# Marks of scores unlike the threshold, made by GpSimd in two passes ahead of use instead of by VectorE in one

## The chip, the core and the metric

The kernel runs on one core of a Trainium2 chip. The metric is the device time of one execution in microseconds (us), the median over runs. In the profile PE is TensorE's matmul, PEld its weight load, DVE is VectorE, ACT is ScalarE and POOL is GpSimd; a name such as L1752 is a line of the kernel.

## The reference, cut to what matters

Two transformer-like blocks follow one another on one sequence of 1024 tokens, width 1024, in float32. The change lies in the first, in its sparse attention. An indexer gives each pair of query and key a score; each query keeps the 256 keys of highest score among those not after it (`lax.top_k`, which takes the earlier key where scores are equal), and softmax attention of 8 heads runs over those keys alone:

```python
score = jnp.where(causal[None], score, -jnp.inf)
_, idx = lax.top_k(score, topk)                  # topk = 256
sel_ok = idx <= t_pos[None, :, None]
kg = jax.vmap(lambda kb, ib: kb[ib])(k, idx)     # the kept keys, vg likewise
logits = jnp.einsum('btkgd,btjkd->btkgj', qg, kg) * (HEAD_DIM ** -0.5)
p = jax.nn.softmax(jnp.where(sel_ok[...], logits, -jnp.inf), axis=-1)
o = jnp.einsum('btkgj,btjkd->btkgd', p, vg)
```

A second branch, the gated one, gives the other half of the features; both halves are normalised, joined and go through the output projection and a feed-forward network of width 4096.

## The kernel before

`select_and_gate` finds the threshold of every query by a search over its bits and leaves it in `found`, one column for each of the six query blocks in `SCORED = [7, 6, 5, 4, 3, 2]`. A query block is 128 queries; block b sees (b + 1) * 128 keys, so the six have 1024, 896, 768, 640, 512 and 384 keys. Blocks 1 and 0 need no selection.

`attend` then does the attention. It works through `order = [1] + SCORED + [0]`, eight blocks of eight heads, as 64 steps (block, head), two steps at a time. Each engine has its own program of these steps, and semaphores join them:

- TensorE, for the pair p: the `logits` of both heads into PSUM (two steps share four banks, so those of steps i wait for the masking of steps i - 2), `turn` (transposes of the probabilities of pair p - 1, which reuse a PSUM bank that VectorE or ScalarE must have copied out), a quarter of the `values` product of the block before, and at set pairs the transposes `by_token` and `turn_y` of a finished block. In the first four pairs it also sums the squares of the gated branch (`sum_gated`, L1651).
- VectorE, in `mask(i)` (L1771), adds the block's row of `never` to the logits, scales, and takes the row's extreme; it copies the transposed probabilities of odd steps out of PSUM (L1814), and it does the selection, `select(j, part)`, one part a step during block j of the order, one block before the block's own masks: part 0 counts scores above the threshold (L1746), part 1 makes in `equal` a mark for each score unlike the threshold (L1749), part 2 runs a scan over these marks that ranks the ties (L1752), parts 3 and 4 (L1754, L1757) turn rank and score into the block's row of `never`. Its other work on a block that is through: `divide`, `mean`, `scale` (L1796), `store`. All of it stands in one queue.
- ScalarE takes the exponentials (L1692) and copies the even steps' transposed probabilities.
- GpSimd multiplies the gated branch by its gain (four instructions, L1572) and by its inverse root (four, L1578), and raises each block's mean square to the power -0.5 (L1584). VectorE's `scale(a)` waits for that power. `mean(a)` comes right behind `select(a + 2, 4)` in VectorE's queue, `scale(a)` one step later, behind one copy of probabilities.

`equal` is one buffer for all six blocks. `wait_ties(eng, a)` waits until part 4 of the selection `a` has run. A barrier stands between attention and the next stage (at 470 us).

Of the kernel before, what the change touches and what calls it, by code (L numbers as in the profile page):

```python
# [15 lines left out]
P = 128  # L16
# [25 lines left out]
AWAY = -2.0 ** 100  # L42

F32 = mybir.dt.float32
# [1414 lines left out]
def attend(nc, K, rot, val, never, found, out, gated):  # L1459
# [29 lines left out]
    with ExitStack() as ctx:  # L1489
# [11 lines left out]
        power = K.sbuf(ctx, "power", [P, 1])  # L1501
        away = K.sbuf(ctx, "away", [P, 1])
        (logits_ready, logits_masked, exp_done, p_turned, copied_by_act, copied_by_dve, pv_ready, y_evicted, y_by_token,
         sum_inverted, y_made, y_squared, mean_made, inverted, y_scaled, y_turned, y_stored, power_set, gain_taken) = (K.flag(n).sem for n in (
             "logits_ready", "logits_masked", "exp_done", "p_turned", "p_copied_by_act", "p_copied_by_dve", "pv_ready",
             "y_evicted", "y_by_token", "sum_inverted", "y_made", "y_squared", "y_mean_made", "y_inverted", "y_scaled",
             "y_turned", "y_stored", "power_set", "gated_gain_taken"))
        psum = K.psum
        p_copied = (copied_by_act, copied_by_dve)
        gated_squares = turned[:, 1].rearrange("p k g j t -> p (k g j t)")[:, 0:4 * S].rearrange("p (t s) -> p t s", t=4)  # L1510
# [22 lines left out]
                return []  # L1533
            return [n for n in range(bank_of[(i, 0)], last_bank[i] + 1) if copier(n) == who]

        tie_steps, before_ties = 6, K.dve_done.n + 1

        def wait_ties(eng, a):

# [21 lines left out]
        with nc.Block(no_gpsimd_drain=True) as block:  # L1561
            @block.gpsimd
            def _(pool):
                for h in range(2):
                    half = gated[:, 3, h * HALF:(h + 1) * HALF]
                    pool.tensor_tensor(out=half, in0=out[:, 0, h * HALF:(h + 1) * HALF], in1=half, op=ALU.mult) \
                        .then_inc(K.pool_done.sem, 1)
                pool.memset(power[:], -0.5).then_inc(power_set, 1)
                wait_ties(pool, 0)
                for t in range(4):  # L1570
                    pool.wait_ge(gated_squared.sem, gated_squared.n + t + 1)
                    pool.tensor_scalar(gated[:, t, :], gated[:, t, :], K.col("g_out_sgu", t), None, op0=ALU.mult) \  # L1572
                        .then_inc(gain_taken, 1)
                pool.wait_ge(gated_rooted.sem, gated_rooted.n + 2)
                wait_ties(pool, 1)
                for t in range(4):
                    pool.wait_ge(gain_taken, t + 1)
                    pool.tensor_tensor(out=gated[:, t, :], in0=gated[:, t, :], in1=gated_root, op=ALU.mult) \  # L1578
                        .then_inc(gated_normed.sem, 1)
                pool.wait_ge(power_set, 1)  # L1580
                for a in range(NT):
                    m = ms[:, a % 2:a % 2 + 1]
                    pool.wait_ge(mean_made, a + 1)
                    pool.tensor_tensor(out=m, in0=m, in1=power[:], op=ALU.pow).then_inc(inverted, 1)  # L1584

# [149 lines left out]
            @block.vector  # L1735
            def _(dve):
                c = Chain(dve, K.dve_done)
                selected = []
                c(dve.memset(away[:], AWAY))

                def select(j, part):

                    s, n = never[:, score_at(SCORED[j]):score_at(SCORED[j] + 1)], (SCORED[j] + 1) * P
                    found_j, same, at = found[:, j:j + 1].bitcast(F32), equal[:, 0:n], rank[:, 0:n]
                    if part == 0:
                        c(dve.tensor_scalar(above[:, 0:n], s, found_j, None, op0=ALU.is_gt, op1=ALU.add,  # L1746
                                            accum_out=count[:]))
                    if part == 1:
                        c(dve.tensor_scalar(same, s, found_j, AWAY, op0=ALU.not_equal, op1=ALU.mult))  # L1749
                    if part == 2:  # L1750
                        c(dve.tensor_scalar(need[:], count[:], -AWAY, AWAY * TOPK, op0=ALU.mult, op1=ALU.add))
                        c(dve.tensor_tensor_scan(at, away[:].broadcast_to([P, n]), same, 0.0, ALU.add, ALU.subtract))  # L1752
                    if part == 3:
                        c(dve.scalar_tensor_tensor(out=same, in0=at, scalar=need[:], in1=same, op0=ALU.subtract,  # L1754
                                                   op1=ALU.min))
                    if part == 4:
                        c(dve.scalar_tensor_tensor(out=s, in0=s, scalar=found_j, in1=same, op0=ALU.is_le, op1=ALU.mult))  # L1757
                        selected.append(c.n)
                        assert c.n == before_ties + tie_steps * (j + 1)

                def mask(i):
                    b, u = steps[i]
                    a, n = i // HEADS, (b + 1) * P
                    if u == 0 and b in SCORED:
                        c.wait(selected[a - 1])
                    dve.wait_ge(logits_ready, i + 1)
                    if i == 2:
                        dve.wait_ge(K.pool_done.sem, K.pool_done.n)
                    if i >= COPIES:
                        dve.wait_ge(p_turned, last_bank[i - COPIES] + 1)  # L1770
                    dve.tensor_tensor_reduce(out=logit[:, i % COPIES, 0:n], in0=keys(logit_banks(i)[0], n),  # L1771
                                             in1=never[:, score_at(b):score_at(b + 1)], scale=-HD ** -0.5,
                                             scalar=3.0e38, op0=ALU.add, op1=ALU.min,
                                             accum_out=low[:, a % 2, u:u + 1]).then_inc(logits_masked, 1)

                def divide(a):
                    dve.wait_ge(exp_done, HEADS * (a + 1))
                    dve.reciprocal(total[:, a % SUMS, :], total[:, a % SUMS, :]).then_inc(sum_inverted, 1)
                    dve.wait_ge(y_by_token, a + 1)
                    dve.wait_ge(sum_inverted, a + 1)  # L1780
                    if a >= 2:
                        dve.wait_ge(y_turned, a - 1)
                    dve.tensor_tensor(out=y[:, a % 2], in0=psum[:, VALUES + a % 2, :].rearrange("p (h d) -> p h d", d=HD),
                                      in1=total[:, a % SUMS, :].unsqueeze(2).broadcast_to([P, HEADS, HD]), op=ALU.mult) \
                        .then_inc(y_made, 1)

                def mean(a):
                    m = ms[:, a % 2:a % 2 + 1]
                    dve.wait_ge(y_squared, a + 1)
                    dve.tensor_scalar(m, m, 1.0 / (HEADS * HD), EPS, op0=ALU.mult, op1=ALU.add).then_inc(mean_made, 1)  # L1790

                def scale(a):
                    m = ms[:, a % 2:a % 2 + 1]
                    dve.wait_ge(inverted, a + 1)
                    flat = y[:, a % 2].rearrange("p h d -> p (h d)")
                    dve.tensor_scalar(flat, flat, m, None, op0=ALU.mult).then_inc(y_scaled, 1)  # L1796

                def store(a):
                    b = order[a]
                    dve.wait_ge(y_turned, a + 1)  # L1800
                    dve.tensor_tensor(out=out[:, :, b * P:(b + 1) * P],
                                      in0=psum[:, VALUES + a % 2, :].rearrange("p (j t) -> p j t", t=P),
                                      in1=K.col("g_out_attn", 0, 4).unsqueeze(2).broadcast_to([P, 4, P]),
                                      op=ALU.mult).then_inc(y_stored, 1)

                for i in range(len(steps) + 10):
                    if i < len(steps) and i % 2 == 0:
                        mask(i)
                        mask(i + 1)
                    if i % 2:  # L1810
                        for n in copies_of(i - 2, 1):
                            to, of = turned_bank(n)
                            wait_turned(dve, n)
                            dve.tensor_copy(to, of).then_inc(copied_by_dve, 1)  # L1814
                    if i // HEADS < len(SCORED):
                        select(i // HEADS, i % HEADS)
                    for a in due(i, DIVIDE, HEADS):
                        divide(a)
                    for a in due(i, MEAN, HEADS):
                        mean(a)  # L1820
                    for a in due(i, SCALE, HEADS):
                        scale(a)
                    for a in due(i, STORE, HEADS):
                        store(a)
                K.dve_done.n = c.n
# [4023 lines left out]
```

## Time and profile before

| | |
|---|---|
| median of 3 runs | 2730.77 us (2730.49 to 2733.97) |
| the profiled execution, its own time | 2734.42 us |
| its span | 2732.7 us |
| mean granted TensorE clock | 0.996 |
| busy: PE, PEld, DVE, ACT, POOL | 2653.1, 2098.8, 1877.9, 1336.1, 264.2 us |
| attention (`attend`) | 323 to 470 us of the span |
| busy there: PE, DVE, ACT, POOL | 137.23, 115.86, 89.53, 27.82 us of 147 |

The time of an execution is the span and 1.7 us around it. Busy shares are averages over stages with different limits; what a change in attention is worth is read from attention's own stretch. Ends of matmuls are modelled, so a busy PE is not PE at its peak. In a row of the timeline the bracket gives the idle time just before, and who ended it.

### The profile page before, as it was taken

The numbers are of one execution on the slowest core, as the hardware profiler recorded it, in microseconds if no ns is written. First come the engines' busy times: TensorE is split into PE (matmuls) and PEld (weight loads), VectorE is DVE, ScalarE is ACT, GpSimd is POOL, SyncE is SP. The second block draws the span as 40 slices with busy tenths as digits, with TensorE's granted clock in tenths as the row PEclk, the third lists the DMA queues.
The fourth block names the chain that finished last, engine by engine and source line by source line (L and its number), as shares of the span: only waits on it lengthen the run. The fifth ranks groups of instructions, "written<-read, shape, count | busy, mean of one in ns | idle before, by whom it ended". The sixth has DMA issues, their size and how long they took to land.

```text
span 2732.7 us, 41783 instructions
## 1 busy us (share of the span) xinstructions
PE 2653.1 (97%) x16684; PEld 2098.8 (77%) x16684; DVE 1877.9 (69%) x2861; ACT 1336.1 (49%) x1979; POOL 264.2 (10%) x390
## 2 busy tenths in 40 slices
PE   7999999999999999999999999989999999999998
PEld 4758755877888888867778898768788878888886
DVE  7889887568665476784987616767565666646676
ACT  4359665587555434464441115453334655543444
POOL 0126520011000000000000002110000100000000
PEclk9999999999999999999999999999999999999999
DMA  7621101365666888722464332216344656687874
GB/s 292 223 89 35 41 1 38 133 213 191 229 231 225 304 284 293 257 110 66 132 163 134 139 131 87 80 45 199 105 149 159 219 201 231 227 303 257 298 279 153
DMA packets 211121, 474.39 MB, mean 174 GB/s; under 512 B 49712, under 2 KB 70832, under 8 KB 205648
## 3 DMA queue, kind: packets, MB, share of 16 engines
q1 hardware_dynamic: 193392, 394.91, 43.7%
q0 software_dynamic: 17536, 76.82, 7.1%
q8 instruction: 132, 2.16, 0.3%
q14 instruction: 61, 0.50, 0.1%
HBM read 344.09 MB, written 124.29 MB: 171 GB/s over the span
## 4 chain that ended last, share of the span: by engine, by line
PE 73%; DVE 5%; ACT 2%; issue 2%; SPq 1%; DMA 1%; ACTq 0%; DVEq 0%
PE psum L2335 44%; PE psum L3890 11%; PE psum L2273 4%; PE psum L5470 3%; PE psum L4301 3%; PE psum L4961 2%; PE psum L4370 1%; PE psum L2281 1%; PE psum L3898 1%; SPq L5169 1%; DMA g_a<-ssm_gate_dram 1%; DVE merged L2887 0%; DVE x L2891 0%; PE psum L2260 0%; PE psum L4435 0%
## 5 line engine op out<-in xcount | busy, mean ns | idle before, releaser
L2335 PE MATMUL psum<-merged_operand 128*128 128x512 f32 x1536 | 360.8, 390 | 0.0
L2335 PEld LDWEIGHTS psum<-merged_operand 128*128 128x128 f32 x1536 | 288.5, 188 | 60.5
L2335 PE MATMUL psum<-h_half_operand 128*128 128x512 f32 x1344 | 316.8, 391 | 0.0
L2335 PEld LDWEIGHTS psum<-h_half_operand 128*128 128x128 f32 x1344 | 252.4, 188 | 55.3 <-issue 1.0
L2335 PE MATMUL psum<-h_half_operand,weight_parts_operand 128*128 128x512 f32 x768 | 177.8, 392 | 0.9 <-DVE weight_parts_operand L2859 0.6
L2335 PEld LDWEIGHTS psum<-h_half_operand,weight_parts_operand 128*128 128x128 f32 x768 | 143.5, 188 | 34.5 <-DVE weight_parts_operand L2859 3.3
L3890 PE MATMUL psum<-x_operand,weight_high 128*128 128x512 f32 x432 | 135.6, 395 | 0.0
L2859 DVE TENSOR_TENSOR weight_parts_operand<-weight_ring,weight_parts_operand 128x1024 fp32r<-128x1024 f32 x65 | 79.5, 1222 | 80.7 <-ACT weight_parts_operand L2501 80.5
L3890 PE MATMUL psum<-o_operand,weight_high 128*128 128x512 f32 x432 | 133.5, 390 | 0.0
L3890 PE MATMUL psum<-x_operand,weight_low 128*128 128x512 f32 x432 | 133.1, 389 | 0.0
L2859 DVE TENSOR_TENSOR h_half_operand<-hidden_upper,h_half_operand 128x1024 fp32r<-128x1024 f32 (+1 forms) x58 | 74.1, 1297 | 72.7 <-ACT h_half_operand L2636 51.9
L2859 DVE TENSOR_TENSOR h_half_operand<-o,h_half_operand 128x1024 fp32r<-128x1024 f32 (+1 forms) x58 | 74.1, 1297 | 71.8 <-ACT h_half_operand L2636 51.0
L2859 DVE TENSOR_TENSOR merged_operand<-o,merged_operand 128x1024 fp32r<-128x1024 f32 (+1 forms) x50 | 64.3, 1309 | 59.9 <-ACT merged_operand L2636 53.2
L2501 ACT ACTIVATE weight_parts_operand<-weight_ring 128x1024 fp32r<-128x1024 f32 x61 | 64.4, 1056 | 81.0 <-PE psum L2273 41.2
L2859 DVE TENSOR_TENSOR merged_operand<-hidden_upper,merged_operand 128x1024 fp32r<-128x1024 f32 (+1 forms) x50 | 64.3, 1308 | 57.4 <-ACT merged_operand L2636 51.0
L3890 PEld LDWEIGHTS psum<-x_operand,weight_high 128*128 128x128 f32 x432 | 79.7, 188 | 28.6 <-issue 13.2
L2335 PE MATMUL psum<-x_operand,merged_operand 128*128 128x512 f32 x384 | 93.4, 392 | 1.4 <-issue 1.4
L3890 PEld LDWEIGHTS psum<-x_operand,weight_low 128*128 128x128 f32 x432 | 81.1, 188 | 17.3
L3890 PEld LDWEIGHTS psum<-o_operand,weight_high 128*128 128x128 f32 x432 | 81.1, 188 | 17.0
L1351 DVE TENSOR_SCALAR_CACHE_REDUCE above<-score,test_bits 128x768 uint8<-128x768 f32 (+3 forms) x114 | 88.1, 826 | 7.3 <-DVE test_bits L1377 7.3
L2335 PE MATMUL psum<-x_operand,h_half_operand 128*128 128x512 f32 x384 | 92.4, 390 | 0.0
L215 DVE CAST weight_high<-weight_ring 128x1024 fp32r<-128x1024 f32 (+1 forms) x43 | 25.5, 594 | 95.0 <-PE psum L3890 58.9
(689 smaller groups left out, 5935.4 us busy)
## 6 DMA issues: line engine op xcount, KB each, us to landing
o<-in_w_ff SPq DMA_DIRECT2D x80, 512.0 KB, 4.5
merged<-hidden_terms SPq DMA_DIRECT2D x56, 512.0 KB, 6.0
hidden_upper<-in_w_ff_down SPq DMA_DIRECT2D x48, 512.0 KB, 4.7
weight_ring<-in_w_out SPq DMA_DIRECT2D x32, 512.0 KB, 3.4
hidden_terms<-weight_parts POOLq DMA_DIRECT2D x16, 1024.0 KB, 8.0
hidden_terms<-weight_ring POOLq DMA_DIRECT2D x16, 1024.0 KB, 7.6
hidden_upper<-in_w_ff_up SPq DMA_DIRECT2D x32, 512.0 KB, 4.6
o<-hidden_terms SPq DMA_DIRECT2D x28, 512.0 KB, 5.9
```

The source lines that it names most:

```text
L1351: counted[j % 2] = c.step(dve.tensor_scalar(above[:, j % 2, 0:(SCORED[j] + 1) * P], keys(j), limit, None, op0=op, op1=ALU.add, accum_out=c ...
L2273: mm = pe.matmul(mix_bank(i), w[:, at], h, start=(k == 0 and m == 0), stop=(k == KT - 1 and m == 2))
L2281: return pe.matmul(mix_bank(i), w[:, k * P:(k + 1) * P], h, start=start, stop=stop)
L2335: mm = pe.matmul(bank, w[:, at:at + P], tiles(r, i), start=opens and m == 0, stop=closes and m == 2, skip_group_check=resumed)
L2501: act.activation(w_high(n), K.ring[:, n % RING, :], ACT.Copy).then_inc(w_rounded.sem, 1)
L2859: return dve.tensor_tensor(out=low, in0=of, in1=plain(high), op=ALU.subtract)
L3890: mm = pe.matmul(banks(n)[:, g, :], w[:, cols], x[:, k, at(g)], start=(k == 0 and m == 0), stop=(k == KT - 1 and m == 2))
L3898: mm = pe.matmul(banks(n)[:, g, :], w[:, cols], x[:, k, at(g)], start=(k == 0 and m == 0), stop=(k == KT - 1 and m == 2))
L4301: mm = pe.matmul(out(k, odd, j), left(k, odd, j), moving(k, odd, j), start=True, stop=True)
L4370: mm = pe.transpose(psum[:, 2, j * P:(j + 1) * P], flat(T[:, n % 2, 2 * j:2 * j + 2, :]), K.const("ident"))
L4961: mm = pe.matmul(K.psum[:, m, :], x[:, k, j:S:BLOCK], w[:, :, at], start=(i == 0 and part == 0), stop=(i == KT - 1 and part == 2))
L5470: return pe.matmul(acc(n)[:, h, :], left[:, n % 2, k * P:(k + 1) * P], x[:, k, h * HALF:(h + 1) * HALF], start=first, stop=last)
```

## The change

VectorE's part 1 (L1749) goes. GpSimd gets a function `mark_unlike(j)` of two dependent passes over the block's scores: the first writes 0 where the score is the threshold and -1 elsewhere, the second multiplies by `-AWAY`, which gives the same marks. It waits for the selection j - 1 to have ended, since `equal` is one buffer, and VectorE's part 2 waits for the second pass. In GpSimd's queue the calls for j = 0 and 1 stand ahead of the gain's multiplications, j = 2 ahead of the root's, and j = 3, 4, 5 each ahead of the power for a = 0, 1, 2. VectorE's selection now counts five instructions instead of six.

```diff
-        tie_steps, before_ties = 6, K.dve_done.n + 1
+        tie_steps, before_ties = 5, K.dve_done.n + 1
...
             @block.gpsimd
             def _(pool):
+                def mark_unlike(j):
+                    if j:
+                        wait_ties(pool, j - 1)
+                    s, n = never[:, score_at(SCORED[j]):score_at(SCORED[j] + 1)], (SCORED[j] + 1) * P
+                    pool.tensor_scalar(equal[:, 0:n], s, found[:, j:j + 1].bitcast(F32), 1.0, op0=ALU.is_equal,
+                                       op1=ALU.subtract).then_inc(unlike_marked, 1)
+                    pool.wait_ge(unlike_marked, 2 * j + 1)
+                    pool.tensor_scalar(equal[:, 0:n], equal[:, 0:n], -AWAY, None, op0=ALU.mult).then_inc(unlike_marked, 1)
+
...
                 pool.memset(power[:], -0.5).then_inc(power_set, 1)
-                wait_ties(pool, 0)
+                mark_unlike(0)
+                mark_unlike(1)
                 for t in range(4):
                     pool.wait_ge(gated_squared.sem, gated_squared.n + t + 1)
                     pool.tensor_scalar(gated[:, t, :], gated[:, t, :], K.col("g_out_sgu", t), None, op0=ALU.mult) \
                         .then_inc(gain_taken, 1)
                 pool.wait_ge(gated_rooted.sem, gated_rooted.n + 2)
-                wait_ties(pool, 1)
+                mark_unlike(2)
...
                 for a in range(NT):
                     m = ms[:, a % 2:a % 2 + 1]
+                    if a + 3 < len(SCORED):
+                        mark_unlike(a + 3)
                     pool.wait_ge(mean_made, a + 1)
                     pool.tensor_tensor(out=m, in0=m, in1=power[:], op=ALU.pow).then_inc(inverted, 1)
...
-                    if part == 1:
-                        c(dve.tensor_scalar(same, s, found_j, AWAY, op0=ALU.not_equal, op1=ALU.mult))
                     if part == 2:
+                        dve.wait_ge(unlike_marked, 2 * j + 2)
                         c(dve.tensor_scalar(need[:], count[:], -AWAY, AWAY * TOPK, op0=ALU.mult, op1=ALU.add))
                         c(dve.tensor_tensor_scan(at, away[:].broadcast_to([P, n]), same, 0.0, ALU.add, ALU.subtract))
```

## Rows read from the trace of the kernel before

**Rows 1.** Windows of attention: us, busy time and instructions of each engine, granted clock, DMA.
```profile
360.00:376.00 16.00, 16.00 (x95) 8.48 (x94) 15.07 (x26) 10.86 (x22) 5.04 (x3) 1.00 0.00 1
```

**Rows 2.** Waits in attention: who waited for whom, us, times, longest.
```profile
DVE p_turned_sbuf L1814 <- PE psum L1613: 9.7, 12, 1.9
...
PE psum L1613 <- DVE p_turned_sbuf L1814: 1.4, 2, 0.8
```

**Rows 3.** GpSimd's groups by shape: count, busy us, mean ns, idle before.
```profile
L1249 POOL TENSOR_SCALAR marks<-score,test_bits 128x384 f32<-128x384 f32 x10 | 12.5, 1249 | 12.4 <-DVEq L1434 12.4
L1572 POOL TENSOR_SCALAR merged<-merged,cols 128x1024 f32<-128x1024 f32 x4 | 11.3, 2839 | 8.2 <-DVE score L1757 8.2
...
L4850 POOL COPY t<-eye 128x512 f32<-128x512 f32 x8 | 5.3, 668 | 3.7 <-PE psum L4301 3.7
```

**Rows 4.** Line 1749 on VectorE: count, shortest/median/longest ns, first and last start.
```profile
L1749 DVE TENSOR_SCALAR equal<-score,found_bits x6: 408/578/1558, 326.1 to 425.2; 128x1024 f32<-128x1024 f32 x1, 128x896 f32<-128x896 f32 x1, 128x768 f32<-128x768 f32 x1, 128x640 f32<-128x640 f32 x1
```

**Rows 5.** GpSimd's timeline early in attention: start, us, operation, idle before.
```profile
325.52 0.10 POOL L1568 MEMSET power<- 128x1 f32 x1
333.81 11.31 POOL L1572 TENSOR_SCALAR merged<-merged,cols 128x1024 f32<-128x1024 f32 x4 [8.19 <-DVE score L1757]
355.68 9.37 POOL L1578 TENSOR_TENSOR merged<-merged,q_k_qi_ki 128x1024 f32<-128x1024 f32 x4 [10.56 <-issue]
376.51 0.59 POOL L1584 TENSOR_TENSOR mean_square<-mean_square,power 128x1 f32<-128x1 f32 x1 [11.47 <-DVE mean_square L1790]
```

**Rows 6.** VectorE's timeline, first block to be selected.
```profile
327.57 0.15 DVE L1751 TENSOR_SCALAR ties_needed<-count 128x1 f32<-128x1 f32 x1
327.76 2.29 DVE L1752 TENSOR_TENSOR_SCAN rank<-away,equal 128x1024 f32<-128x1024 f32 x1
```

**Rows 7.** TensorE's timeline, 330 us: two transposes of probabilities.
```profile
330.65 0.41 PE L1613 MATMUL psum<-consts,q_k_qi_ki 128*128 128x128 f32 x2 [0.85 <-DVE p_turned_sbuf L1814]
```

**Rows 8.** VectorE's timeline, 375 to 419 us: selection, scaling, last mask, three times.
```profile
375.17 1.01 DVE L1757 SCALAR_TENSOR_TENSOR score<-score,found_bits,equal 128x768 f32<-128x768 f32 x1
...
377.37 0.48 DVE L1796 TENSOR_SCALAR y_by_token<-y_by_token,mean_square 128x512 f32<-128x512 f32 x1
...
378.77 1.08 DVE L1771 CUSTOM_DVE_ANT_0 q_k_qi_ki<-psum,score 128x896 f32<-128x896 f32 x1
...
396.10 0.88 DVE L1757 SCALAR_TENSOR_TENSOR score<-score,found_bits,equal 128x640 f32<-128x640 f32 x1
...
398.03 0.48 DVE L1796 TENSOR_SCALAR y_by_token<-y_by_token,mean_square 128x512 f32<-128x512 f32 x1
...
399.30 0.95 DVE L1771 CUSTOM_DVE_ANT_0 q_k_qi_ki<-psum,score 128x768 f32<-128x768 f32 x1
...
415.04 0.75 DVE L1757 SCALAR_TENSOR_TENSOR score<-score,found_bits,equal 128x512 f32<-128x512 f32 x1
...
416.71 0.48 DVE L1796 TENSOR_SCALAR y_by_token<-y_by_token,mean_square 128x512 f32<-128x512 f32 x1
...
418.00 0.82 DVE L1771 CUSTOM_DVE_ANT_0 q_k_qi_ki<-psum,score 128x640 f32<-128x640 f32 x1
```

**Rows 9.** TensorE's timeline, the logits after each of those masks.
```profile
381.24 1.56 PE L1599 MATMUL psum<-q_k_qi_ki 64*128 64x512 f32 x8
...
401.90 1.35 PE L1599 MATMUL psum<-q_k_qi_ki 64*128 64x512 f32 x8
...
419.99 1.13 PE L1599 MATMUL psum<-q_k_qi_ki 64*128 64x512 f32 x4
```

**Rows 10.** Timeline at 1619 us: GpSimd, then VectorE with two SBUF inputs.
```profile
1618.66 2.35 POOL L4856 TENSOR_TENSOR a_off_diagonal<-pairs_and_ends,chunk_consts 128x1024 f32<-128x1024 f32 x1 [3.08 <-DVE pairs_and_ends L4684]
...
1619.31 2.28 DVE L4701 COPY_PREDICATED t<-chunk_consts,a_low 128x512 f32<-128x512 uint32 x1
```

**Rows 11.** TensorE, three windows: us, busy (instructions), granted clock, DMA share, GB/s.
```profile
342.00:348.00 6.00, 2.64 (x17) 0.95 0.00 0
...
348.00:351.00 3.00, 3.00 (x12) 0.52 0.03 5
```

More of the change, by code:

```diff
@@ L1503, in attend @@
         (logits_ready, logits_masked, exp_done, p_turned, copied_by_act, copied_by_dve, pv_ready, y_evicted, y_by_token,
-         sum_inverted, y_made, y_squared, mean_made, inverted, y_scaled, y_turned, y_stored, power_set, gain_taken) = (K.flag(n).sem for n in (
+         sum_inverted, y_made, y_squared, mean_made, inverted, y_scaled, y_turned, y_stored, power_set, gain_taken, unlike_marked) = (K.flag(n).sem for n in (
              "logits_ready", "logits_masked", "exp_done", "p_turned", "p_copied_by_act", "p_copied_by_dve", "pv_ready",
              "y_evicted", "y_by_token", "sum_inverted", "y_made", "y_squared", "y_mean_made", "y_inverted", "y_scaled",
-             "y_turned", "y_stored", "power_set", "gated_gain_taken"))
+             "y_turned", "y_stored", "power_set", "gated_gain_taken", "unlike_marked"))
         psum = K.psum
```

## The prediction

> **What bounds the kernel now.** I read the page first, then attention alone, because the change touches nothing outside 323 to 470 us: its windows, its waits, GpSimd's groups by shape, and the timelines of VectorE, TensorE and GpSimd at the places where a wait is added. In the window of a middle block TensorE is busy throughout, 16.00 of 16 us, and VectorE 15.07 [rows 1]. TensorE's matmuls stand there end to end, so it sets the pace and VectorE follows with little to spare. The waits say the same: VectorE's copies wait 9.7 us for TensorE's transposes, and TensorE waits for such a copy twice, 1.4 us in all [rows 2], one of them the 0.85 us at 330.65 [rows 7]. The barrier behind attention lets nothing overlap, so a microsecond that TensorE loses here is lost at the end. What matters is where VectorE becomes late enough for TensorE to feel it.
>
> **What is removed.** Six marks on VectorE, 408 to 1558 ns with a median of 578 [rows 4]; by the six single times 4.35 us together. All but the first lie where TensorE does not wait for VectorE, so I cost them at nothing; their cover is TensorE's own queue. The bound on the other side is 1 us, for a little slack gained.
>
> **What one pass costs on GpSimd.** The trace has no such two-operation pass. The nearest are the comparison with a per-partition operand over 384 elements, 1249 ns, and the multiplication over 1024, 2839 ns [rows 3]. A line through both is 2.48 ns an element and 0.30 us. By it a pass over 1024, 640, 512 and 384 elements takes 2.84, 1.88, 1.57 and 1.25 us, and the two with 0.1 us between them 5.8, 3.9, 3.2 and 2.6 us. From below, the nearest is the copy of 512 elements at 0.668 us [rows 3], some 1.2 ns an element, if an immediate operand made a pass that cheap. From above I allow the first pass, with two operations, half as much again. I take the line, since both its rows are this very kind of instruction.
> The Trainium skill speaks for the low end: "GPSIMD Engine Reference", section 4.1, has GpSimd at about line rate for one-input work. At one element a cycle of its 1.2 GHz that would be an estimated 0.85 us for 1024 elements; both rows of the kind contradict it by a factor near three.
>
> **Term 1, the first block.** GpSimd's queue reaches the marks behind the memset, at 325.6 us [rows 5]. Two passes of 1024 end at 331.4. VectorE's part 2 then needs 0.2 us for its small instruction, and the scan starts at 331.65 instead of 327.76 [rows 6]: 3.9 us later, with the removed mark already counted. "One block ahead" holds from the second block on; the first has no block before it. Queued behind the waiting part are the copy of step 1, parts 3 and 4, and the masks of steps 4 and 5. TensorE's transpose at 330.65 waits for that very copy [rows 7], so it is late by the same amount, and everything behind it on three engines. From 3.9 us the bounds are 0.5 (both passes as the copy) and 5.3.
>
> **Term 2, the power behind the marks.** For a = 0, 1, 2 GpSimd must now do `mark_unlike(a + 3)` before the power, and may start it only when selection a + 2 has ended. VectorE's `scale(a)` waits for the power and comes one step behind that selection. For a = 0 the selection ends at 376.2 and `scale` starts at 377.37 [rows 8]. GpSimd would start at 376.3, mark until 380.15, and give the power (0.59 us before [rows 5]) at 380.8: VectorE stands 3.4 us. For a = 1 the selection ends at 397.0, the power comes at 400.95 and `scale` was due at 398.03: 2.9 us. For a = 2 it is 415.8, 419.1 and 416.71: 2.4 us [rows 8].
> Behind `scale` in VectorE's queue stand the two masks whose banks the next logits need. The second of them ends at 379.86, 400.26 and 418.83 with its readout [rows 8]; TensorE's next logits start at 381.24, 401.90 and 419.99 [rows 9], the ones for the second bank 0.15 us later. The slack is 1.5, 1.8 and 1.3 us, and TensorE loses 1.9, 1.1 and 1.1: 4.1 us. At later transposes and copies VectorE is then late by no more than TensorE is. Bounds: 0 (passes as the copy: the first stall is 1.2 us, under its slack) and 6.5 (the two-operation pass half as long again adds 0.9, 0.8 and 0.6).
> The marks for j = 1 to 5 are themselves ready before their scans: for j = 1 at 343 against a scan near 350, the tightest of them, so that added wait costs nothing there. If it did, it would be the scan's delay one for one.
>
> **Term 3, two engines at one port.** A VectorE instruction with two SBUF inputs at 1619 us started 0.65 us behind one of GpSimd's and ended 0.6 us after it; its 2.28 us for 512 elements [rows 10] are twice what the scan takes for an element [rows 6] and seem to be some 1.7 us of standing until GpSimd was through, and 0.6 of work. Before, the gain's four instructions ran at 333.8 to 345.1 and the root's at 355.7 to 365.05 [rows 5], clear of scans. Now they come behind marks: the gain's at about 343 to 354, the root's at about 365 to 375. All of VectorE's clock is then some 5 us later, so the scans of the second and third block, at 346 and 368 before, fall near 351 and 373.5, inside both. Each can be held 0 to 2.8 us. The second block has an idle microsecond behind it; the third has 0.4 us of slack, read as in term 2. I take 1.0 us, bounds 0 and 3.
> The Trainium skill has this as a rule: "SBUF — State Buffer" calls the shared port pair an exclusive lock, held for the whole instruction, and names two SBUF inputs against a GpSimd instruction that reads. The trace agrees, by those 2.28 us.
>
> **Term 4, TensorE's clock.** From 342 to 348 us TensorE was busy only 2.64 of 6 us, and from 348 to 351 its granted clock was 0.52, so 1.2 GHz for most of 3 us, before it rose again to 2.4 [rows 11]. Term 1 makes a new hole, from about 329.8 to 334.6, busy some 1.2 of 6 us around it. I expect the same fall behind it: 3 us at half rate, 1.5 us lost. Bounds: 0 (no fall) and 3.5 (one more behind a stall of term 2).
>
> **The sum.** 3.9 + 4.1 + 1.0 + 1.5 - 0 = 10.5 us. Against the profiled execution's own 2734.42 us that is 2744.9; that execution is 3.65 us over the median of the runs, 2730.77, and against the median it gives 2741.3 us. The other bounds, not all at once, reach from about +1 to about +17.
>
> **The rivals.** A change under 0.2% (5.5 us) can't be told from none here.
> (a) Main: GpSimd's marks cost about as the line says, and the four waits bite; +6 to +16 us, most likely +10.5, 2741.3 us. Chance 0.72.
> (b) Only the second pass, with an immediate, runs at the copy's rate. Each pair is 0.75 to 1.6 us shorter: term 1 is 2.3, term 2 about 1.4, terms 3 and 4 together 1: +4.7, 2735.5 us. For it: no row shows an immediate pass of this size. Against: a comparison and a multiplication cost much the same an element, 3.3 and 2.8 ns with all overheads [rows 3], so what the pass does seems not to matter. Chance 0.11, half of it within 0.2%.
> (c) Both passes near the copy's rate, 1.2 ns an element. Term 1 is 0.6, term 2 nothing, the rest nothing: 2731.4 us, no change. This is the case on the other side; it decides once a pass of 1024 takes less than about 2 us, where terms 1 and 2 together fall to some 3. By the rule of "GPSIMD Engine Reference" of the Trainium skill, named above, this is the case that comes out. Against it stand both rows of the kind. Chance 0.06. A gain over 0.2% would want more than the 4.35 us removed, so it gets 0.02, for a clock fall at 348 us that the new timing spares as well.
> (d) The two-operation pass costs half as much again, or the clock falls after several stalls, or VectorE is held at the port each time: +16 to +22, say 2750 us. Chance 0.09.
>
> **Range and chances.** From 2735 to 2748.5 us; outside it lie (c), the faster case, most of (d), and a tail of (b). Slower by over 0.2%: (a) nearly whole, (d), half of (b): 0.87. Within: 0.11. Faster: 0.02.
>
> **What would show it.** The waits of the profile after should have VectorE waiting for GpSimd's `equal` once, some 4 us, and for `mean_square` three times, 2.4 to 3.4 us each; the marks' groups on GpSimd give the pass's price at once (2.84 us for 1024). The granted clock should fall near 335 us. The barrier should come some 10 us later, and the stages behind it keep their lengths. I am wrong if a pass of 1024 takes much under 2 us (b, c), or if TensorE's idle time in attention grows by much less than VectorE's stalls, which would mean more slack than I read.

## The result and the profile after

The changed kernel takes 2744.92 us in the median of 6 runs (2742.05 to 2751.25), the one before 2732.05 (2730.49 to 2735.29): ratio 1.0047, 95% interval 1.0035 to 1.0059, so 12.8 us slower (9.6 to 16.1). The prediction said 10.5 us slower, 2741.3 us. Its other figure, 2744.9, was counted from the one profiled execution, and that the median came out at the same number is chance; 1.3 of the 3.6 us between 2741.3 and 2744.92 is that the kernel before came out slower in six runs than in the three it was counted from.

The first two lines of the page after, and its busy line: GpSimd has 28.5 us more to do, VectorE 2.7 us less, TensorE the same work.

```profile
span 2740.3 us, 41788 instructions
...
PE 2654.6 (97%) x16684; PEld 2098.1 (77%) x16684; DVE 1875.2 (68%) x2855; ACT 1335.9 (49%) x1979; POOL 292.7 (11%) x402
```

Those 2740.3 us are the span of the fastest of the six runs. It is not the span that tells what the change did, but attention's own length. TensorE's first and last logits there, before and then after (an extract of each timeline: start, duration, what; the bracket is idle time before):

```profile
323.25 0.70 PE L1599 MATMUL psum<-q_k_qi_ki 64*128 64x256 f32 x4 [1.33 <-PEq L1023]
```

```profile
455.90 0.49 PE L1599 MATMUL psum<-q_k_qi_ki 64*128 64x128 f32 x4
```

```profile
321.11 0.70 PE L1611 MATMUL psum<-q_k_qi_ki 64*128 64x256 f32 x4 [1.33 <-PEq L1023]
```

```profile
465.92 0.49 PE L1611 MATMUL psum<-q_k_qi_ki 64*128 64x128 f32 x4
```

From 132.65 to 144.81 us: 12.16 us longer. Attention began 2.1 us earlier in this trace, and what follows it was 2.4 us shorter. Both lie in code that the change does not touch: the start is taken up below, and what follows differs by 3.3 us between the two traces of the kernel before itself.

The waits in attention, as in [rows 2] (who waited for whom: us, times, longest). Two are new, VectorE for GpSimd's marks (`equal`) and for its power (`mean_square`), and TensorE's wait for VectorE's copies has grown from 1.4 to 6.8 us:

```profile
DVE y_by_token L1807 <- POOL mean_square L1596: 10.4, 5, 3.9
...
PE psum L1625 <- DVE p_turned_sbuf L1825: 6.8, 3, 5.5
...
DVE ties_needed L1762 <- POOL equal L1571: 5.4, 1, 5.4
...
PE psum L1656 <- DVE y_by_token L1807: 1.6, 3, 1.1
```

GpSimd's groups by shape, beside [rows 3] (busy us, mean ns, idle before). L1568 is the first pass, with two operations, L1571 the second, L1582 the gain's multiplication:

```profile
L1582 POOL TENSOR_SCALAR merged<-merged,cols 128x1024 f32<-128x1024 f32 x4 | 12.1, 3042 | 0.1
...
L1568 POOL TENSOR_SCALAR equal<-score,found_bits 128x1024 f32<-128x1024 f32 x1 | 3.7, 3721 | 0.0
...
L1571 POOL TENSOR_SCALAR equal<-equal 128x1024 f32<-128x1024 f32 x1 | 2.8, 2793 | 0.1
...
L1568 POOL TENSOR_SCALAR equal<-score,found_bits 128x640 f32<-128x640 f32 x1 | 2.4, 2431 | 7.9 <-DVE score L1768 7.9
...
L1571 POOL TENSOR_SCALAR equal<-equal 128x640 f32<-128x640 f32 x1 | 1.8, 1816 | 0.1
```

VectorE's timeline where it now waits, beside [rows 6, 8]: the scans of the first three blocks, and the three scalings:

```profile
330.10 0.15 DVE L1762 TENSOR_SCALAR ties_needed<-count 128x1 f32<-128x1 f32 x1 [5.37 <-POOL equal L1571]
330.29 2.29 DVE L1763 TENSOR_TENSOR_SCAN rank<-away,equal 128x1024 f32<-128x1024 f32 x1
...
349.68 2.02 DVE L1763 TENSOR_TENSOR_SCAN rank<-away,equal 128x896 f32<-128x896 f32 x1
...
371.13 3.65 DVE L1763 TENSOR_TENSOR_SCAN rank<-away,equal 128x768 f32<-128x768 f32 x1
...
386.09 0.48 DVE L1807 TENSOR_SCALAR y_by_token<-y_by_token,mean_square 128x512 f32<-128x512 f32 x1 [3.94 <-POOL mean_square L1596]
...
408.67 0.48 DVE L1807 TENSOR_SCALAR y_by_token<-y_by_token,mean_square 128x512 f32<-128x512 f32 x1 [3.26 <-POOL mean_square L1596]
...
428.38 0.49 DVE L1807 TENSOR_SCALAR y_by_token<-y_by_token,mean_square 128x512 f32<-128x512 f32 x1 [2.57 <-POOL mean_square L1596]
```

TensorE behind the first and the second of these waits, beside [rows 7, 9]:

```profile
333.18 0.66 PE L1625 MATMUL psum<-consts,q_k_qi_ki 128*128 128x128 f32 x2 [5.52 <-DVE p_turned_sbuf L1825]
333.64 3.62 PE L1663 MATMUL psum<-p_turned_sbuf,consts 128*128 128x512 f32 x4
...
386.63 0.66 PE L1656 MATMUL psum<-consts,y_by_token 128*128 128x128 f32 x4 [1.06 <-DVE y_by_token L1807]
387.63 2.57 PE L1611 MATMUL psum<-q_k_qi_ki 64*128 64x512 f32 x8 [0.35 <-DVE minus_max L1782]
```

And its windows (us, busy, granted clock, DMA share, GB/s), beside [rows 11]:

```profile
328.00:332.00 4.00, 0.00 (x0) 1.00 0.01 2
333.00:339.00 6.00, 5.82 (x13) 0.50 0.00 0
347.00:353.00 6.00, 2.64 (x21) 1.00 0.00 0
```

Below, a hole is a stretch in which TensorE stands idle, and a fall is one in which its granted clock is 0.50, 1.2 GHz. The reader can follow the loss by the start of each pair's logits, less the first one's, against the same difference before. It is nothing up to the third pair. At the sixth pair it is 6.7 us: the scan came 4.7 us late, TensorE stood 5.52 us at the transpose, and came out of the hole at 1.2 GHz, 0.50 for six microseconds, in which the 512-wide sums at 333.64 took 3.62 us. Then 1.6 us come back: the fall at 348 us before [rows 11] is missing. The third block's scan, 3.65 us where its length is 1.76, adds 1.0 us. The three scalings add 3.5, 1.7 and 1.0. From there on the difference stays 12.15 us to the last logits.

### The profile page after: what moved, and what is told of

Same layout as the page of the kernel before. It is cut to its first block, busy times and chain, and to the rows that moved or that the text cites. A ratio compares the mean times of both kernels' runs of the same rounds, so it can differ in the third digit from the quotient of the medians.

```text
span 2740.3 us, 41788 instructions
## 1 busy us (share of the span) xinstructions
PE 2654.6 (97%) x16684; PEld 2098.1 (77%) x16684; DVE 1875.2 (68%) x2855; ACT 1335.9 (49%) x1979; POOL 292.7 (11%) x402
## 4 chain that ended last, share of the span: by engine, by line
PE 75%; DVE 4%; ACT 2%; issue 1%; ACTq 0%; DVEq 0%
PE psum L2346 44%; PE psum L3901 11%; PE psum L2284 4%; PE psum L5481 3%; PE psum L4312 3%; PE psum L4972 2%; PE psum L5197 1%; PE psum L2292 1%; PE psum L4381 1%; PE psum L3909 1%; DVE merged L2898 0%; DVE x L2902 0%; PE psum L2271 0%; PE psum L4446 0%; PE psum L4436 0%
## 5 line engine op out<-in xcount | busy, mean ns | idle before, releaser
L2346 PEld LDWEIGHTS psum<-h_half_operand,weight_parts_operand 128*128 128x128 f32 x768 | 143.5, 188 | 34.5 <-DVE weight_parts_operand L2870 3.3
```

The source lines that it names most:

```text
L2346: mm = pe.matmul(bank, w[:, at:at + P], tiles(r, i), start=opens and m == 0, stop=closes and m == 2, skip_group_check=resumed)
```

## The experiments

The measure in them is attention's length, from its first logits to its last, by one trace each; the ratio of whole runs stands beside it with its interval. A trace is one execution of several, and need not be a typical one: where the two columns disagree, the text says so.

| kernel | attention, us | against before | ratio of whole runs (95%) |
|---|---|---|---|
| before; again | 132.65; 132.65 | 0 | |
| changed; again; a third time | 144.81; 144.62; 144.65 | +12.16; +11.97; +12.00 | 1.0047 (1.0035 to 1.0059) |
| first block's marks by VectorE; again | 143.46; 138.15 | +10.81; +5.50 | 1.0043 (1.0026 to 1.0060) |
| power ahead of marks | 139.35 | +6.70 | 1.0025 (1.0012 to 1.0037) |
| both | 132.75 | +0.10 | 1.0002 (0.9991 to 1.0012) |
| one pass | 135.87 | +3.22 | 1.0016 (1.0005 to 1.0026) |
| hole filled | 145.43 | +12.78 | 1.0064 (1.0050 to 1.0078) |
| port alone | 136.47 | +3.82 | 1.0020 (1.0010 to 1.0029) |
| before, holes filled | 131.16 | -1.49 | 1.0006 (0.9996 to 1.0017) |
| relief alone | 132.63 | -0.02 | 1.0012 (1.0002 to 1.0021) |

**The first block's marks by VectorE again.**

```diff
-                mark_unlike(0)
...
+                    if part == 1 and j == 0:
+                        c(dve.tensor_scalar(same, s, found_j, AWAY, op0=ALU.not_equal, op1=ALU.mult))
                     if part == 2:
-                        dve.wait_ge(unlike_marked, 2 * j + 2)
+                        if j:
+                            dve.wait_ge(unlike_marked, 2 * j)
```

> The changed kernel, but VectorE makes the marks of the first block itself, as before, so that GpSimd starts with the second. Theory (the waits for GpSimd are the loss, term by term): the stall of 4.7 us at the first scan and the fall of the clock behind it (2.1 us) go, and the fall near 348 us comes back (1.6 us): attention 7.1 us longer than before instead of 12.15. Rival one (the two engines hold each other up at their shared port, wherever GpSimd works beside VectorE): nearly the same GpSimd work is left, so 10 us or more stay.

Up to the sixth pair the starts are those of before: the stall at the scan is gone, as expected. But 10.8 us stayed in this trace, by the clock and not by the port. Its windows show two falls, one 2.5 us ahead of the place of the old one and for 7 us, and one behind the scaling's stall of 3.9 us, which cost 3.2 us more there than the changed kernel lost:

```profile
351.10:355.10 4.00, 3.89 (x14) 0.50 0.02 4
391.10:395.10 4.00, 4.00 (x14) 0.50 0.00 0
```

> Once more the kernel in which VectorE makes the first block's marks. In its first trace attention was 10.8 us longer than before, where 7.1 were expected, with a stretch at 1.2 GHz near 390 us behind the stall of 3.9 us. Theory (that fall wanders): without a fall there, attention is 6 to 8 us longer; with one, 10 to 12. Rival (the stall before the scaling always brings the clock down when nothing fell before it): the same fall at the same place, 10.8 us.

The second trace of the same kernel has no fall in attention at all, and every step but the clock's is the same. It is 5.5 us over before, which had its fall of 1.6 us: 7.1 us where neither falls. That is the 7.1 expected at first; the 6 to 8 us expected of this trace were missed, since they took for granted that the fall near 348 us would be there. Whole runs are on the side of the first trace: the six of this kernel took 2742.2 to 2749.9 us, 1.0043, no better than the changed kernel's 1.0047, and the execution of the second trace, at 2736.25 us, is faster than all of them. So this edit takes away the first stall, and in most executions the clock seems to take the gain back; one trace shows where, and no run shows how often.

```profile
340.00:350.00 10.00, 6.64 (x41) 1.00 0.01 2
380.00:390.00 10.00, 9.53 (x50) 1.00 0.00 0
```

**Each power ahead of the marks.**

```diff
                 for a in range(NT):
                     m = ms[:, a % 2:a % 2 + 1]
-                    if a + 3 < len(SCORED):
-                        mark_unlike(a + 3)
                     pool.wait_ge(mean_made, a + 1)
                     pool.tensor_tensor(out=m, in0=m, in1=power[:], op=ALU.pow).then_inc(inverted, 1)
+                    if a + 3 < len(SCORED):
+                        mark_unlike(a + 3)
```

> The changed kernel, but in GpSimd's last loop each power stands ahead of the marks, not behind them. Theory: the three stalls of 3.9, 3.3 and 2.6 us before the scaling go, with the 6.1 us that TensorE lost by them; the first block's stall and the clock stay: attention 6.1 us longer than before, the scaling never waits for GpSimd over 0.5 us. Rival one (shared port): the marks then run beside VectorE's scaling and copies instead of while it stands still, and 10 us or more stay.

Measured +6.7 us, 5.3 to 5.5 less than the changed kernel's three traces, and whole runs agree (1.0025 is 6.8 us). The waits for the scaling are back at 0.6 us, and the marks are still ready in time:

```profile
DVE ties_needed L1762 <- POOL equal L1571: 5.4, 1, 5.4
...
DVE y_by_token L1807 <- POOL mean_square L1594: 0.6, 2, 0.4
```

It is 0.6 us over the expected 6.1. The starts say why: the third block's scan now costs TensorE 1.75 us (1.0 at once, 0.75 a pair later), where it seemed to cost 1.0 in the changed kernel. The rest had eaten slack that the scaling's stall then missed.

**Both edits.**

> Both edits: VectorE makes the first block's marks, and each power stands ahead of the marks. Theory: what is left is the scan held at the port, 1 us (0 to 3), so within 0.2% of before, and no gain from the 3 us of VectorE's work removed, since TensorE sets the pace. Rival one (shared port): over 5 us slower. Rival two (VectorE's relief is worth something once the stalls are gone): 2 to 3 us faster than before.

+0.10 us, and a ratio of one. In this trace nothing falls near 348 us, so the sum is 1.63 us gained by the clock and 1.75 us lost at the third block's scan. That scan took 3.68 us here and in the kernel above, 1.76 us before; GpSimd's root multiplications (L1587) ran beside it:

```profile
366.18 3.68 DVE L1765 TENSOR_TENSOR_SCAN rank<-away,equal 128x768 f32<-128x768 f32 x1
```

```profile
358.89 9.35 POOL L1587 TENSOR_TENSOR merged<-merged,q_k_qi_ki 128x1024 f32<-128x1024 f32 x4
```

**One pass.**

```diff
-                    pool.wait_ge(unlike_marked, 2 * j + 1)
-                    pool.tensor_scalar(equal[:, 0:n], equal[:, 0:n], -AWAY, None, op0=ALU.mult).then_inc(unlike_marked, 1)
...
-                        dve.wait_ge(unlike_marked, 2 * j + 2)
+                        dve.wait_ge(unlike_marked, j + 1)
```

> The changed kernel without GpSimd's second pass, so the marks are 0 and -1 and the selection is not the reference's; durations don't hang on the values. Theory: the first block's marks take 3.7 us instead of 6.6, the scan is 1.8 us late instead of 4.7, the stalls before the scaling are 2.0, 1.7 and 1.3 us instead of 3.9, 3.3 and 2.6, nearly all within TensorE's slack: 1.8 + 1.3 + 1 = some 4 us longer than before, 6 if the clock falls behind the first stall. Rival one (shared port): half of GpSimd's added work is gone, so half of 12 us, 6 us. Rival three (a fixed cost of the handover, not the pass, makes the stalls): stalls shrink by less than 1 us each and 10 us stay.

+3.2 us: 1.8 at the first scan, 0.9 from a fall at 353 us, at the same two holes as the old one, that lasted 7 us instead of 3, and 0.5 at the scalings. All three stalls there fell to 1.9, 1.55 and 1.2 us, by the length of the pass left out and 0.2 us, and two of them cost nothing:

```profile
387.65 0.49 DVE L1805 TENSOR_SCALAR y_by_token<-y_by_token,mean_square 128x512 f32<-128x512 f32 x1 [1.92 <-POOL mean_square L1594]
...
408.53 0.49 DVE L1805 TENSOR_SCALAR y_by_token<-y_by_token,mean_square 128x512 f32<-128x512 f32 x1 [1.55 <-POOL mean_square L1594]
...
426.91 0.49 DVE L1805 TENSOR_SCALAR y_by_token<-y_by_token,mean_square 128x512 f32<-128x512 f32 x1 [1.19 <-POOL mean_square L1594]
```

The third block's scan took its 1.76 us: with one pass less in front, GpSimd's root multiplications ended at 376.3 us, 0.3 before it. A fixed cost of the handover is ruled out, since the stalls shrank by 2.0, 1.7 and 1.4 us where it allowed less than 1, and the port's 6 us did not come.

**The hole filled.**

```diff
+                    if p == 2:
+                        K.stay_busy(pe, LOGITS + 1, 20)
                     if 1 <= p <= pairs:
                         turn(2 * p - 1)
```

> The changed kernel, with 20 short matmuls of constants into an unused bank between the two transposes at which TensorE stands 5.5 us, so that it stands less than 1 us. Theory (the hole brings the clock down): the granted clock stays at 2.4 GHz at 333 to 339 us; the 2.1 us lost there are saved; the stall itself stays. A fall near 348 us may come back, at 1.6 us. Attention 10.1 to 11.7 us longer than before, and the runs spread less than the 9 us of the changed kernel's. Rival four (the clock falls by itself, the hole has no part): still at half rate for several us near 335, no less spread.

The first half came out exactly: TensorE waits 1.05 us, the clock stays up, and the fourth to sixth pairs are 4.66 us late, not 6.6. That is the stall by itself.

```profile
336.28 4.63 PE L174 MATMUL psum<-consts 128*128 128x128 f32 x40
341.96 0.41 PE L1625 MATMUL psum<-consts,q_k_qi_ki 128*128 128x128 f32 x2 [1.05 <-DVE p_turned_sbuf L1827]
```

```profile
337.90:341.90 4.00, 3.01 (x27) 1.00 0.00 2
357.90:361.90 4.00, 3.24 (x12) 0.50 0.00 0
```

The second half did not: the clock now fell at the next holes, near 358 us, for 7 us, and with 12.8 us nothing was saved. The whole runs were slower still, 1.0064 or 17.5 us, of which this trace's attention shows 12.8; the expected smaller spread (5.4 us against 9) rests on five runs.

**The port alone.**

```diff
-                wait_ties(pool, 0)
...
-                wait_ties(pool, 1)
```

> The kernel before, with nothing of the change, only without GpSimd's two waits for the selections ahead of the gain's and of the root's multiplications, so that these run beside VectorE's instructions with two SBUF inputs: the gain's at 326 to 338 us, the root's from 347 us. It measures the port alone. Theory (whoever comes second stands until the other's instruction has ended): the first block's scan and its two following instructions are held 1 to 2.8 us each while TensorE waits for what is behind them: 2 to 5 us longer than before, scans in the trace 1 to 2.8 us over their lengths. Rival five (they share the port at some common rate): GpSimd's instructions too are longer where they overlap, VectorE's by less than half, 0 to 1 us longer in all.

+3.8 us, in the expected range, a part of it a longer fall at 348 us. The first scan was not held. The instructions behind it were, by less than expected in the first block: L1752 took 1.62 and L1755 2.09 us, where their length is 1.27 and 1.28. In the second block both took some 3.0 us, where it is 1.14 and 1.15. VectorE's timeline, then GpSimd's, each instruction by itself; the lines are that kernel's, two less than in the kernel before:

```profile
327.42 2.29 DVE L1750 TENSOR_TENSOR_SCAN rank<-away,equal 128x1024 f32<-128x1024 f32 x1
...
332.44 2.09 DVE L1755 SCALAR_TENSOR_TENSOR score<-score,found_bits,equal 128x1024 f32<-128x1024 f32 x1
...
350.75 3.00 DVE L1752 SCALAR_TENSOR_TENSOR equal<-rank,ties_needed,equal 128x896 f32<-128x896 f32 x1
```

```profile
325.86 3.38 POOL L1571 TENSOR_SCALAR merged<-merged,cols 128x1024 f32<-128x1024 f32 x1 [0.61 <-ACT p_turned_sbuf L1719]
...
332.34 2.84 POOL L1571 TENSOR_SCALAR merged<-merged,cols 128x1024 f32<-128x1024 f32 x1
...
350.46 2.34 POOL L1576 TENSOR_TENSOR merged<-merged,q_k_qi_ki 128x1024 f32<-128x1024 f32 x1
```

GpSimd lost too: its two sets took 12.14 and 10.68 us, 11.31 and 9.37 before [rows 5]. But its two kinds of work behave differently. Beside the root's multiplications, which read two large inputs, whichever came second stood until the other was through: one ran from 350.46 to 352.80, and L1752, begun at 350.75, ended 0.95 us behind it; the multiplication after that took 3.22 us instead of 2.37. Beside the gain's, which read one, VectorE was let through early: L1755 began 0.10 us behind one of 2.84 us and was held for only 0.8, and the first scan, begun 1.56 us into one, was not held at all. The same shows in the kernel before, where the second block's mark (L1749) began 0.03 us behind a gain's multiplication and took 1.56 us, 0.9 more than its size asks for [rows 4]:

```profile
342.27 2.84 POOL L1572 TENSOR_SCALAR merged<-merged,cols 128x1024 f32<-128x1024 f32 x1
```

```profile
342.30 1.56 DVE L1749 TENSOR_SCALAR equal<-score,found_bits 128x896 f32<-128x896 f32 x1
```

So the theory holds for the root's and not for the gain's. The rival was right that GpSimd pays too, and its "by less than half" fits only L1752 in the first block. Why the gain's lets VectorE through no run shows.

**Relief alone.**

```diff
-                    if part == 1:
+                    if part == 1 and j == 0:
```

> The kernel before, in which VectorE makes the marks of the first block only and nobody makes the others: the selections of the other five blocks work on stale marks, so the output is not the reference's; durations don't hang on the values. It is the relief of VectorE alone, 3.6 us of its work, with no wait and no work added on GpSimd. Theory (TensorE sets the pace, so the relief is worth nothing): attention the same within 0.3 us, but for a fall of the clock near 348 us that comes or not (1.6 us). Rival two (the relief is worth what it frees): 2 to 3.6 us shorter beyond that.

Every start of logits is that of before within 0.03 us but one, 0.27 us early beside the fall of the clock, which is there as before. The 3.6 us of VectorE, five of its six marks, are worth nothing in this trace. The ratio of whole runs, 1.0012, is not explained by it: the traced execution is the second fastest of its eleven, 4.4 us under their median, and no trace shows where the others lose. A gain of 2 to 3.6 us they rule out.

**The clock.** Five traces ask whether its falls are the program's.

> The kernel before once more, for a second trace. Theory (the fall of the clock near 348 us wanders): the fall is missing, and attention 1.6 us shorter, or there for 3 to 7 us; elsewhere every step of TensorE is the same within 0.1 us. Rival (it is fixed by the program): the same 3 us at half rate.

> The changed kernel once more, for a second trace of it. Theory (stalls and port are fixed by the program, the clock's falls wander from run to run): up to the clock the steps at which TensorE falls behind are the same within 0.1 us (4.66 at the first scan, 1.0 at the third block's scan), each stall before the scaling 3.9, 3.3 and 2.6 us, and the stretches at 1.2 GHz lie elsewhere or have another length; attention 11 to 17 us longer than before. Rival (the clock falls at the same places of the program each time): at half rate from 332 to 339 us and nowhere else.

> The changed kernel a third time, with the same expectations as for its second trace.

> The kernel before, with 7 and 6 short matmuls of constants where TensorE stands 1.80 and 1.56 us ahead of 344.7 and 347.4 us, so that it hardly stands at all. Theory (those two holes bring the clock down near 348 us): the granted clock stays at 2.4 GHz from 342 to 352 us and attention is 1.6 us shorter than before; too little to tell by the times of whole runs. Rival (the fall at 348 us has another cause): the clock still falls there, attention the same within 0.3 us.

The kernel before fell again at the same place, so there the rival was right. The changed one fell at the same place all three times, so there too it was the rival that was right; attention's 12.0 us and the stalls repeated, which both had expected. It fell behind the 5.5 us hole, where the power-first kernel with the same hole fell too. Near 348 us, at two holes of 1.80 and 1.56 us, the clock fell in the two traces of before and in those of port alone, one pass, relief alone, the hole filled and one of the two with VectorE's first marks, and did not in both edits, in the other of these two, nor in any with the 5.5 us hole. The same program shows both, so that fall can wander, though most programs here have one trace only. It began behind both holes in the two traces of before and in relief alone, and lasted 3 us; in the other four it began before TensorE was through the second, and lasted 7. Filling its holes in the kernel before gave 1.49 us, but both edits were spared with the holes open; it is not shown that the filling did it. That trace is also the fastest of twelve executions, and whole runs show no gain, 1.0006 (0.9996 to 1.0017). Behind attention's end, outside the measure, every trace but this one has one more fall of some 3 us. The changed kernel again:

```profile
340.00:345.00 5.00, 4.99 (x10) 0.50 0.00 0
362.00:372.00 10.00, 9.66 (x60) 1.00 0.00 0
```

## Why the prediction was right, point by point

**TensorE sets the pace, VectorE's relief is nothing.** Shown for five of the six marks: 0.0 us of attention by relief alone. The first mark's removal stands in term 1.

**A pass on GpSimd.** The second, 2.79 and 1.82 us for 1024 and 640 elements, lies on the line (2.84 and 1.88). The first, 3.72 and 2.43 us, does not: two operations cost 3.3 ns an element, not 2.5. The comparison is not dear by itself: alone it took 1.25 us for 384 elements [rows 3], with the subtraction 1.59. "Half as much again" had been the upper bound; it was 0.3. The rivals with cheap passes fell by this alone.

**Term 1, the first block: 3.9 us predicted, 4.66 measured** by the filled hole. The mechanism held to the copy behind the scan; the missing 0.8 us is the dearer first pass.

**Term 2, the powers: 4.1 predicted, some 5.3 measured** by putting them first (5.3 to 5.5 against the changed kernel's three traces). The stalls are 3.94, 3.26 and 2.57 us for 3.4, 2.9 and 2.4. The 1.1 us that this adds went through whole, since the slack had been used already. The slack itself, read off the next masks and logits, was right within 0.3 us for each, as far as the port's share can be taken apart. One dependence I had not named: TensorE's transpose of the scaled block waits directly for the scaling (L1656, 1.06 us); the logits behind it waited longer, so it changed nothing.

**Term 3, the port: 1.0 predicted.** It looks like 1.0 in the changed kernel but is 1.75 where nothing follows that could hide it. The third block's scan was held as foreseen, 1.9 us: it began at 371.13, behind a root's multiplication that ran from 370.80 to 373.17, and ended 1.61 us after that. The second block's, foreseen too, was not, and there the mechanism of the prediction is wrong for one kind of GpSimd's work. That scan began at 349.68 in the middle of the third of the gain's multiplications and still took its 2.02 us; the fourth stood instead, and the four together took 12.10 us for 11.31. GpSimd's timeline, each instruction by itself:

```profile
347.89 2.84 POOL L1582 TENSOR_SCALAR merged<-merged,cols 128x1024 f32<-128x1024 f32 x1
...
350.71 3.64 POOL L1582 TENSOR_SCALAR merged<-merged,cols 128x1024 f32<-128x1024 f32 x1
...
370.80 2.37 POOL L1588 TENSOR_TENSOR merged<-merged,q_k_qi_ki 128x1024 f32<-128x1024 f32 x1
```

The Trainium skill's "SBUF — State Buffer" says that the one that starts first keeps the pair for the whole instruction. The trace agrees for the third block's scan, 3.65 us against 1.76, and for the fourth multiplication, 3.64 against 2.84, which came behind the scan. It does not agree for the second block's scan, which by that rule would have stood 1.05 us, until 350.73.

**Term 4, the clock: 1.5 predicted, +2.1 and -1.6 measured.** The fall behind the new hole came in every trace and was longer, six to seven microseconds for three. That the old one would be missing then I had left to a case of 2 in 100; in all three traces it was.

**The sum.** 10.5 predicted for attention, 12.0 to 12.2 measured; the step that was mis-sized is the price of the two-operation pass, which enters terms 1 and 2. Two errors of terms 3 and 4, +0.75 and -1.0 us, nearly cancel, and that is luck. Why whole runs differ by more than attention: in three traces of the same changed kernel attention began at 321.1, 328.0 and 329.1 us, while the granted clock from 10 to 60 us was 1.00, 0.90 and 0.86. The median of the runs holds that too, and agrees with attention's 12 us within its interval.

By whole runs no version here beats the kernel before: both edits only come back to it, since what VectorE gives up is worth nothing.

## What to carry to other kernels

Ask of work that is moved to an idle engine what else stands in that engine's queue behind it: here the marks were free only where the next item was not wanted at once, and one swap of two lines gave back 5.3 of 12 us. "Ahead of use" must hold for the first block as well. And before an engine is relieved, leave its work out in one run: relief alone was 0.0 us of attention.

## What was not expected of the hardware

GpSimd's price hangs on the operations of a pass: 3.3 ns an element with a comparison and a subtraction, some 2.5 with a multiplication. Beside GpSimd's multiplications of two large inputs a VectorE instruction that comes second stands until they end; beside those of one it was held for at most 0.9 us of their 2.84. After a hole of 5.5 us TensorE ran at 1.2 GHz for six to seven microseconds, in four traces of four, and the fall that the kernel before has further on did not follow; where the hole was filled, it did, and longer than before. Falls behind holes of under 2 us come in one run and not in the next of the same program, 3 to 7 us long. Against 12 us of change, that is the noise to reckon with. For the changed kernel attention's own length, read from first to last logits, was steadier (144.6 to 144.8 us in three traces) than the whole run (2742 to 2751 us). With VectorE's first marks it was not: the same program gave 143.5 and 138.2 us, all of it the clock.
